# Loading and splitting the first weights of a layer outside the ring

## The reference

```
x = layer_norm(ALPHA * x + time_mix_or_attention(x)); x = layer_norm(ALPHA * x + swiglu(x))   # layers 0 to 3
x = x + mixer(rmsnorm(x)); x = x + swiglu(rmsnorm(x))                                        # layers 4 to 11
swiglu(h) = (silu(h @ w_gate) * (h @ w_up)) @ w_down                                         # 1024 -> 2816 -> 1024
```

## Time and profile before

| what | us |
|---|---|
| median of three runs | 2048.99 |
| profiled execution, its own time | 2047.56 |
| span of its trace (first to last instruction) | 2045.8 |
| PE busy in the span | 1986.2 |
| DVE busy | 1276.6 |
| ACT busy | 908.8 |
| mean granted PE clock | 0.995 of full |

### The profile page before, as it was taken

One profiled execution on the slowest core, in us unless ns is written; L12 is line 12 of the kernel. 1 busy time (PEld: TensorE's weight loads), 2 busy tenths in 40 slices (PEclk: granted clock), 3 DMA queues, 4 the chain that ended last, 5 costly groups with the idle time before them and its releaser, 6 DMA issues.

```text
span 2045.8 us, 32584 instructions
## 1 busy us (share of the span) xinstructions
PE 1986.2 (97%) x12754; PEld 1615.7 (79%) x12754; DVE 1276.6 (62%) x1623; ACT 908.8 (44%) x1282; POOL 161.6 (8%) x198
## 2 busy tenths in 40 slices
PE   7999999999999999999999999999999999999999
PEld 6689688878678879888878678877766888897887
DVE  7774755477665556655667655577886554575554
ACT  4452354434444434444555454434434444434442
POOL 2252100000010010000003011001100000000000
PEclk9999999999999999999999999999999999999999
DMA  8321265555166554565455257553323555555554
GB/s 302 114 63 45 98 216 182 189 170 180 62 201 200 196 185 165 171 210 184 166 190 191 73 167 226 200 185 124 104 83 126 192 185 187 174 167 187 183 171 155
DMA packets 93040, 335.95 MB, mean 164 GB/s; under 512 B 11230, under 2 KB 11364, under 8 KB 92623
## 3 DMA queue, kind: packets, MB, share of 16 engines
q1 hardware_dynamic: 85824, 311.62, 45.9%
q0 software_dynamic: 7120, 22.95, 3.8%
HBM read 332.43 MB, written 1.05 MB: 163 GB/s over the span
## 4 chain that ended last, share of the span: by engine, by line
PE 87%; DVE 8%; issue 2%; POOL 2%; ACT 2%; DMA 0%; SPq 0%; DVEq 0%; ACTq 0%; POOLq 0%
PE acc L361 42%; PE acc L448 20%; PE acc L419 9%; DVE w_lo L1554 2%; PE acc L920 2%; PE aux L841 1%; PE aux L468 1%; PE aux L625 1%; PE aux L876 1%; POOL rstd L2371 1%; PE aux L908 1%; DVE operand_lo L1575 1%; PE aux L897 1%; ACT w_hi L1169 1%; POOL rstd L2374 1%
## 5 line engine op out<-in xcount | busy, mean ns | idle before, releaser
L1554 DVE TENSOR_TENSOR w_lo<-w_raw,w_hi 128x1024 fp32r<-128x1024 f32 x588 | 716.7, 1224 | 569.5 <-ACT w_hi L1169 562.5
L1169 ACT ACTIVATE w_hi<-w_raw 128x1024 fp32r<-128x1024 f32 x588 | 620.6, 1059 | 786.6 <-PE acc L361 456.4
L361 PE MATMUL acc<-w_hi,operand_hi 128*128 128x512 f32 x1344 | 536.7, 399 | 27.0 <-DVE operand_lo L1720 12.1
L361 PE MATMUL acc<-w_hi,operand_lo 128*128 128x512 f32 x1344 | 526.8, 392 | 0.0
L361 PE MATMUL acc<-w_lo,operand_hi 128*128 128x512 f32 x1344 | 526.3, 392 | 0.0
L361 PEld LDWEIGHTS acc<-w_hi,operand_hi 128*128 128x128 f32 x1344 | 253.6, 189 | 91.8 <-DVE operand_lo L1575 15.4
L361 PEld LDWEIGHTS acc<-w_hi,operand_lo 128*128 128x128 f32 x1344 | 253.5, 189 | 54.0
L361 PEld LDWEIGHTS acc<-w_lo,operand_hi 128*128 128x128 f32 x1344 | 254.0, 189 | 50.3 <-issue 0.5
L448 PE MATMUL acc<-w_hi,hidden_hi 128*128 128x512 f32 x528 | 207.9, 394 | 0.0
L448 PE MATMUL acc<-w_hi,hidden_lo 128*128 128x512 f32 x528 | 205.9, 390 | 0.0
L448 PE MATMUL acc<-w_lo,hidden_hi 128*128 128x512 f32 x528 | 205.6, 389 | 0.0
(11 more groups left out here) (474 smaller groups left out, 2111.7 us busy)
## 6 DMA issues: line engine op xcount, KB each, us to landing
w_raw<-in_weights SPq DMA_DIRECT2D x588, 512.0 KB, 3.4
ln_gain<-in_gains POOLq DMA_DIRECT2D x7, 512.0 KB, 5.0
bias_at<-in_rpb POOLq DMA_DIRECT2D x12, 256.0 KB, 5.1
ln_gain<-in_ln_g POOLq DMA_DIRECT2D x4, 512.0 KB, 3.9
ln_bias<-in_ln_b POOLq DMA_DIRECT2D x4, 512.0 KB, 5.1
vec_rw<-in_vec POOLq DMA_DIRECT2D x3, 512.0 KB, 5.6
l_rw<-in_lora SPq DMA_DIRECT2D x1, 1152.0 KB, 10.6
iclr_rw<-in_xT SPq DMA_DIRECT2D x2, 512.0 KB, 4.6
```

What stands on the lines that cost most here:

```text
L361: mm = pe.matmul(acc[:, 2 * pair + t, :], (ah, al)[x][:, kt, t * P:(t + 1) * P], W[w][:, s, kk * 512:(kk + 1) * 512], start=(kt == 0 and ( ...
L1169: act.activation(whi[:, s, :], raw[:, s, :], ACT.Copy).then_inc(w_hi[s], 1)
L1554: dve.tensor_tensor(wlo[:, s, :], raw[:, s, :], whi[:, s, :].bitcast(F32), ALU.subtract).then_inc(w_lo[s], 1)
```

## The change

Nine of the eleven later layers are `spared`: all but near (6) and hyena (8). Their first four quarters leave the ring. They are loaded into `SPARE_RAW` and split into `SPARE_HI` and `SPARE_LO`, which lie over memory that is dead at that time. The ring goes on with the remaining quarters (`in_ring[q]` counts them). ACT and DVE make the four splits inside the layer before: in the down projection behind rows 6, 9, 12 and 15; in moba behind pairs 4, 5, 6 and 7; in near two behind pair 7 and two inside `residual`; in conv all four ahead of the outgoing projection; in rwkv and hyena two ahead of its other splits and two behind them. Each of ACT's spare splits waits until all four loads have landed (`spare_full`). SP's loop is written out; a spare load waits for what frees its memory. `residual` of a layer ahead of a spared one holds no other splits and has a new order. In `first_block` the filler products go where the quarters are spared.

```diff
+    spared = [n for n, kind in enumerate(layers) if n and kind not in ("near", "hyena")]
+    beside_ring = {start[n] + i: SLOTS * k + i for k, n in enumerate(spared) for i in range(SLOTS)}
+    in_ring = {q: r for r, q in enumerate(q for q in range(quarters) if q not in beside_ring)}
...
+        def load_spare(n, i):                                   # SP
+            if i == 0:
+                sp.wait_ge(m["spare_used"], SLOTS * spared.index(n))
+                if layers[n - 1] == "rwkv":
+                    sp.wait_ge(m["y_ready"], TT)
+                elif layers[n - 1] == "near":
+                    sp.wait_ge(m["scores_ready"], PAIRS * sum(kind in ("moba", "near") for kind in layers[:n]))
+                elif layers[n - 1] == "hyena":
+                    sp.wait_ge(m["operand_ready"], operands(n - 2) + 4)
+            sp.dma_start(raw_of(start[n] + i), A["weights"][start[n] + i]).then_inc(m["spare_full"], 16)
+        def spare_beside(n, k):
+            at = {"ffn": (FB * 4, FB * 4 + 4, FB * 4 + 8, FB * 4 + 12), "conv": (4, 10, 16, 22), "moba": (IN_Q, IN_Q + 1, IN_Q + 2, IN_Q + 3)}
+            at = at.get(layers[n - 1], (IN_Q + OUT_Q - 1,) * SLOTS)
+            for i in range(SLOTS):
+                if at[i] == k:
+                    load_spare(n, i)
...
-                        if src is X:                            # PE, first_block
+                        if src is X and q not in beside_ring:
                             keep_busy((0, 0, 3, 1)[i])
...
         def split(q, at=None):                                  # ACT
+            if q in beside_ring:
+                act.wait_ge(m["spare_full"], 16 * SLOTS * (beside_ring[q] // SLOTS + 1))
+            else:
...                                                              # the ring's waits as before
+            act.activation(weight(0, q), raw_of(q), ACT.Copy).then_inc(hi_of(q)[0], 1)
+        def spare(q, first, n):                                 # ACT and DVE
+            for k in range(first, first + n):
+                if q in beside_ring:
+                    split(q + k)
...
+            early = n + 1 in spared                             # ACT, residual
+            if early:
+                if rms:
+                    square(0)
+                if layers[n] == "near":
+                    split(q + 2)
+                if not channels:
+                    operand(0)
+                if layers[n] == "near":
+                    split(q + 3)
+                if rms:
+                    square(1)
+                if channels:
+                    operand(0)
+                operand(1)
+                return
...
                 centred(0)                                      # DVE, residual, layers 0 to 3
-                if rms:
-                    ahead(q - 4, 1)
                 normed(0)
+                add_with_stats(1, 0)
                 if not rms:
-                    ahead(q - 4, 1)
-                    operand(0, (0,))
-                    ahead(q - 3, 1)
-                    operand(0, (1,))
-                add_with_stats(1, 0)
+                    operand(0)
                 add_with_stats(1, 1)
                 moments(1)
-                if not rms:
-                    ahead(q - 2, 1)
                 centred(1)
-                if not rms:
-                    ahead(q - 1, 1)
                 normed(1)
                 if rms:
                     rms_normed(0)
+                    operand(0)
                     rms_normed(1)
-                    both_operands()
-                    ahead(q - 3, 3)
-                else:
-                    operand(1)
+                operand(1)
                 return
             add(0, 0)                                           # layers 4 to 11
             add(0, 1)
...
+            if layers[n] == "near":
+                split(q + 2)
             rms_normed(0)
+            if early and not channels:
+                operand(0, (0,))
+                add(1, 0)
+                operand(0, (1,))
+                add(1, 1)
+                if layers[n] == "near":
+                    split(q + 3)
+                rms_normed(1)
+                operand(1)
+                return
+            if early:
+                add(1, 0)
+                add(1, 1)
+                operand(0)
+                rms_normed(1)
+                operand(1)
+                return
...
             both_operands()                                     # ACT and DVE, end of rwkv and hyena
+            spare(q + IN_Q + OUT_Q, 0, 2)
             ahead(q + IN_Q, OUT_Q - 4)
+            spare(q + IN_Q + OUT_Q, 2, 2)
...
                 output_hi(p)                                    # ACT, pair loop; DVE has output_lo(p)
                 if 2 <= p <= OUT_Q - 3:
                     split(q + IN_Q + p - 2 + SLOTS)
+                if near and p == PAIRS - 1:
+                    spare(q + IN_Q + OUT_Q, 0, 2)
+                elif not near and p >= SLOTS:
+                    spare(q + IN_Q + OUT_Q, p - SLOTS, 1)
```

More of the change, by code:

```diff
@@ L40 @@
 SLOTS = 4
+SPARE_ROWS = (6, 9, 12, 15)
 QW = 1024
@@ L151, in program @@
         RBT = rwkv("rb_rw", [P, TT, 2, KT, CH])
+        [FM] = scope(("transition_rw", [P, 2, KT, HD]))
+        KTT = rwkv("k_turned", [P, KT, SEQ])
         CUM, SPAN = scope(("cum_rw", [P, 2, P]), ("span_rw", [P, TT, 3]))
@@ L311, in nth, with operands, slot, of @@
     def nth(q, at=None):
-        n = q // SLOTS + 1
+        n = in_ring[q] // SLOTS + 1
         return n if at is None else at[0] * (at[1] // SLOTS) + n
+    def operands(n):
+        return sum({"rwkv": 8, "hyena": 8, "moba": 4 + PAIRS, "near": 4 + PAIRS}.get(kind, 4) for kind in layers[:n + 1])
+    def slot(q):
+        return in_ring[q] % SLOTS
+    def of(sems, spare, q, at=None):
+        return (m[spare], beside_ring[q] + 1) if q in beside_ring else (sems[slot(q)], nth(q, at))
+    def hi_of(q, at=None):
+        return of(w_hi, "spare_hi", q, at)
+    def lo_of(q, at=None):
+        return of(w_lo, "spare_lo", q, at)
+    def used_of(q, at=None):
+        return of(w_used, "spare_used", q, at)
+    def weight(x, q):
+        return (SPARE_HI, SPARE_LO)[x][:, beside_ring[q] % SLOTS, :] if q in beside_ring else W[x][:, slot(q), :]
+    def raw_of(q):
+        return SPARE_RAW[:, beside_ring[q] % SLOTS, :] if q in beside_ring else raw[:, slot(q), :]
     start = {}
@@ L331, in _ @@
         sp.dma_start(XT[:, 4:KT, :], A["xT"][:, 4:KT, :]).then_inc(m["x2_in"], 16)
[L332 to L340, removed]
@@ new lines, in spare_beside @@
+        def spare_beside(n, k):
[4 more added lines that the diff above has]
+                    load_spare(n, i)
+        for n in range(len(layers)):
+            for k in range((start[n + 1] if n + 1 < len(layers) else quarters) - start[n]):
+                q = start[n] + k
+                if q not in beside_ring:
+                    if in_ring[q] >= SLOTS:
+                        sp.wait_ge(w_lo[slot(q)], nth(q) - 1)
+                    sp.dma_start(raw_of(q), A["weights"][q]).then_inc(w_full[slot(q)], 16)
+                if n == 0 and k == SLOTS - 1:
+                    sp.dma_start(L1[:], A["lora1"]).then_inc(m["rwkv_in"], 16)
+                if n + 1 in spared:
+                    spare_beside(n + 1, k)
@@ L439, in project @@
             for n, (kt, t, c) in enumerate(steps):
-                s = (q + kt) % SLOTS
+                s = slot(q + kt)
                 if c == 0 and (kt, t) in before:
@@ L912, in project_part @@
             def project_part(kt, t):
-                s = (q + IN_Q + kt) % SLOTS
+                s = slot(q + IN_Q + kt)
                 if t == 0:
@@ L1212, in residual @@
             if channels:
-                if n >= LAYER_NORMS:
-                    ahead(q - 4, 1)
-                ahead(q - 3, 1)
+                ahead(q - 4, 2)
                 square(1)
@@ L1373, in ffn @@
                         sine(k // 8)
+                    if k in SPARE_ROWS:
+                        spare(q + FFN_Q, SPARE_ROWS.index(k), 1)
                 return
@@ L1559, in ahead, with spare @@
                     split(q + k + SLOTS, at)
+        def spare(q, first, n):
+            for k in range(first, first + n):
+                if q in beside_ring:
+                    split(q + k)
         def used(q, at=None):
-            dve.wait_ge(w_used[q % SLOTS], nth(q, at))
+            dve.wait_ge(*used_of(q, at))
         def step(instruction):
@@ L2559, in norms @@
                     rms_root(t)
-            operands = sum({"rwkv": 8, "hyena": 8, "moba": 4 + PAIRS, "near": 4 + PAIRS}.get(kind, 4) for kind in layers[:n + 1])
             if n + 1 < len(layers):
-                pool.wait_ge(m["operand_ready"], operands)
+                pool.wait_ge(m["operand_ready"], operands(n))
                 if n + 1 < LAYER_NORMS:
```

103 lines of the change are left out of this document (48 added, 55 removed).

## The result

The changed kernel is slower: 2054.83 us as the median of 11 runs (2049.25 to 2058.17) against 2047.53 us for the kernel before (11 runs), ratio 1.0033, 95% interval 1.0022 to 1.0043. The forecast was 2034. "Ratio" is always the time over that of the kernel before, measured beside it. The profiled execution took 2052.27 us, 4.7 more than that of before, which is the difference to explain here; the forecast for it was 14.85 less, so 19.6 us are missing.

The account below looks back on a forecast made before the run. PE was taken as the bound (busy 97%), leaving it mainly at layer passages, where DVE's splits delay it. Passage gains less costs in moba and near summed to -14.85 us: profiled 2032.7, median 2034, eight-in-ten range 2028 to 2042.

Parts of the forecast that it names:

- Passages: Passages into spared layers get shorter: rwkv-ffn -2.65, ffn-moba -3.15, moba-ffn -4.65, conv-ffn -3.3 twice, hyena-ffn -2.6 us.
- Spare splits in moba and near: Spare splits not hidden: moba +2.3 us (behind pairs 4 and 5), near +2.5 with its order and a clock fall.
- The four spare splits at the end of conv: In conv the four (4.9 us) end ahead of the first ring split, which waits for a slot: cost 0.
- SP and the loads. [...] Cost 0: SP's queue: ring loads queue behind waiting spare loads, but their splits come only after the passage: cost 0, closely in near.
- about as many or more in rwkv and hyena: Time from memory release to ACT's first use of spare loads: 11 us in near, about that or more there.
- Rival D: Loads late: ACT waits at its first spare split if four loads take over 11 us; slower, 2050 to 2070; chance 0.06.
- Rival A: Without fillers PE's waits drop the clock in three passages of layers 0 to 2 and ffn to conv: 2040; chance 0.14.
- B: Cost of the spare splits in moba and near is hidden: 2029; chance 0.10.
- C: Passages don't get shorter, as adds, statistics, roots and turns take up what the splits leave: 2045; chance 0.10.

Follow-up runs that it names:

- fillers_back: conv_11_hyena_behind with the four fillers of the first tile put back in the passages into layers 1, 2 and 3; 2049.66 us, ratio 1.0001.
- before_no_fillers: The kernel before with only the four first-tile fillers taken out in the three passages that had them; 2052.27 us, ratio 1.0015.
- hyena_behind: The changed kernel with hyena's four spare splits all behind the ring's four, instead of two ahead and two behind; 2053.17 us, ratio 1.0016.
- moba_behind_6_7: conv_11_hyena_behind with moba's spare splits two behind pair 6 and two behind pair 7, not one each behind pairs 4 to 7; 2036.28 us, ratio 0.9940.
- hyena_not_spared: conv_at_11 with the passage hyena to ffn as in the kernel before; 2037.21 us, ratio 0.9938.
- conv_at_11: The changed kernel with conv's four spare loads at 11, 14, 17, 20 in SP's order instead of 4, 10, 16, 22; 2037.16 us, ratio 0.9948.
- conv_at_6: The changed kernel with conv's first spare load at 6 instead of 4 in SP's order, the others unmoved; 2039.66 us, ratio 0.9957.
- conv_11_hyena_behind: The changed kernel with the edits of both conv_at_11 and hyena_behind; 2035.53 us, ratio 0.9939.

## Why the prediction was wrong

- **Passages: right.** -2.7, -2.7, -4.7, -3.6, -3.4, -2.8 against -2.65, -3.15, -4.65, -3.3, -3.3, -2.6. What I had not said is that in the first three this hangs on both halves of the edit: fillers_back gave back 3.4 in each, and before_no_fillers gained nothing.
- **Spare splits in moba and near: right in kind.** +2.8 against +2.3, +1.2 against +2.5. In near the order cost 0.9 of the 1.0 that I gave it, and the clock fell as I had said, for 0.7 instead of 1.6; the rest of near's stretch won 0.5. That the clock fell was luck: in four of the eight traces with this wait it did not.
- **The four spare splits at the end of conv, costed at 0: nearly.** I had them end ahead of the first ring split. They do, but the ring's splits come right behind them, one by one, and PE waits for three: 0.8 per layer.
- **The step that failed: "SP and the loads. [...] Cost 0".** I had the mechanism in the sentence ahead ("later ring loads queue behind") and dropped it for "those splits come only after the passage". That is so in rwkv, near and hyena, where the spare loads follow the layer's last ring load; in moba and ffn their wait is long over. In conv the first one stands at k = 4 of 32, and what is late is not the spare quarter but ring quarter 5 behind it. I asked only how long the spare loads have until ACT needs them; the question was who stands behind the wait, and when those are due. Price 6.5 + 7.2, of which 0.8 each is not the queue.
- **"about as many or more in rwkv and hyena"** (11 us from release to first use) was read in near alone and carried over. In hyena the release is at 1541.6 and ACT stands at its first spare split from 1540.9, so there is no slack, and four loads take 8.4. Price 4.5 of the 5.5 (the wait and the clock behind it); the 1.0 at the projection's start is the clock's and is there without this cause too.
- **Rival D had the right kind and the wrong condition.** Both of its halves happened: ACT at its first spare split with the ring's splits behind it (hyena), ring loads behind spare loads on SP (conv). I let it decide at four loads over 11 us, a question of bandwidth, and gave it 0.06; they landed in 8.4, and it happened by order alone. That is why slower had only 0.05.
- **Rival A** is real where the fillers go and the splits stay (before_no_fillers, clock 0.57 behind a wait of 3.37), and absent from the same passages of the changed kernel. B and C were not seen.

## What to carry to other kernels

When a load with a wait is put into a queue that works in order, look at each place where it is put: what stands behind it, when that is due, and when the wait can end. The slack of the new load says nothing of this. A slack read at one such place is not that of the others; each needs its two times. Where an engine's wait is covered by fillers, taking out the wait gains little until the fillers go too, and taking out the fillers alone can cost the clock. A difference of a microsecond or two between single traces can be the clock behind a wait that both have; read the granted clock there before naming a cause.

## What the runs showed of the hardware

- Four 512 KB loads issued together landed 8.4 us after the first was issued (1541.68 to 1550.10), about 250 GB/s; a ring load issued 0.4 us behind a spare one took 4.23 (778.02), against a median of 3.4.
- PE stood for 3.37 and 4.16 us and came back at 0.57 of full clock over the next 4 us; in conv 1.5 and 2.3 us were lost beyond the wait (6.5 and 7.2, less 0.8 and the wait), in the passage 1.6 (eight products 0.43 apart instead of 0.23).
- Shorter waits did so in some traces and not in others. The wait of 2.6 us in near was followed by 0.50 of full clock in after, hyena_behind, moba_behind_6_7 and hyena_not_spared, and by 1.00 in conv_at_11, conv_at_6, conv_11_hyena_behind and fillers_back; that of 1.9 us in ffn to conv by 0.57 in before_no_fillers and 1.00 in before.
